# Seven block products instead of eight in the down product of an MLP, with the sums of token tiles made on GpSimd

## The reference, cut to what matters

```
for i in range(2):
    ...
    u = rms_norm(x, g_mlp[i])                                   # 256 x 1024
    x = x + jnp.square(jax.nn.relu(u @ w_ff1[i])) @ w_ff2[i]    # 1024 -> 4096 -> 1024
```

## Time and profile before

| | before |
|---|---|
| median of the runs | 798.21 us |
| the profiled execution, its own time | 798.14 us |
| its span, first to last instruction | 796.3 us |
| PE busy | 789.5 us (99%) |
| PE weight loads busy | 658.7 us (83%) |
| VectorE busy | 530.0 us (67%) |
| ScalarE busy | 425.1 us (53%) |
| GpSimd busy | 106.9 us (13%) |

### The profile page before, as it was taken

The page is one execution under the profiler, slowest core; times in us unless marked ns, Lnnn a source line. Parts: engine busy times, 40 slices in busy tenths (PEclk is TensorE's granted clock), DMA queues, the critical chain, the costliest instruction groups (busy, mean ns, idle before and its releaser), DMA issues.

```text
span 796.3 us, 11076 instructions
## 1 busy us (share of the span) xinstructions
PE 789.5 (99%) x4150; PEld 658.7 (83%) x4150; DVE 530.0 (67%) x709; ACT 425.1 (53%) x615; POOL 106.9 (13%) x136
## 2 busy tenths in 40 slices
PE   8999999999999999999999999999999999999998
PEld 7998977778888778888888888887778888888886
DVE  6657987767676677576655656678766756666561
ACT  6646655654755564464444454548674545534440
POOL 0500300000130410030000000078900000000000
PEclk9999999999999999999999999999999999999999
DMA  9961463447656634546665565461424566656541
GB/s 344 352 201 40 159 198 121 142 156 287 221 196 201 208 106 149 169 158 213 212 208 175 194 207 170 151 212 54 134 79 159 170 215 223 220 178 208 172 144 53
DMA packets 76230, 142.52 MB, mean 179 GB/s; under 512 B 2928, under 2 KB 21504, under 8 KB 76064
## 3 DMA queue, kind: packets, MB, share of 16 engines
q1 hardware_dynamic: 74128, 135.08, 50.9%
q0 software_dynamic: 1776, 6.84, 2.5%
q10 hardware_dynamic: 288, 0.10, 0.0%
HBM read 140.95 MB, written 1.05 MB: 178 GB/s over the span
## 4 chain that ended last, share of the span: by engine, by line
PE 97%; DVE 1%; ACT 1%; DMA 0%; issue 0%; ACTq 0%; DVEq 0%
PE bank L1776 60%; PE bank L2154 15%; PE bank L2160 7%; PE bank L1949 2%; PE bank L2017 2%; PE bank L1864 2%; PE bank L1798 1%; PE bank L1831 1%; PE bank L1917 1%; PE bank L1991 1%; PE bank L2223 1%; PE bank L1790 1%; PE bank L1997 1%; DMA proj<-in_opening 0%; PE bank L2213 0%
## 5 line engine op out<-in xcount | busy, mean ns | idle before, releaser
L1776 PE MATMUL bank<-w_hi,a_both 128*128 128x512 f32 (+2 forms) x720 | 226.3, 384 | 0.1
L1193 DVE TENSOR_TENSOR w_lo<-raw,w_hi 128x2048 fp32r<-128x2048 f32 (+2 forms) x67 | 152.5, 2277 | 63.2 <-ACT w_hi L712 61.5
L1657 DVE TENSOR_TENSOR w_lo<-raw,w_hi 128x2048 fp32r<-128x2048 f32 x48 | 110.0, 2292 | 90.6 <-ACT w_hi L1095 89.6
L2154 PE MATMUL bank<-a_both,w_hi 128*128 128x512 f32 x512 | 163.2, 396 | 0.0
L712 ACT ACTIVATE w_hi<-raw 128x2048 fp32r<-128x2048 f32 (+2 forms) x67 | 125.9, 1879 | 68.0 <-PE bank L1776 31.2
L1776 PEld LDWEIGHTS bank<-w_hi,a_both 128*128 128x128 f32 x720 | 134.6, 188 | 22.0 <-issue 1.7
L1095 ACT ACTIVATE w_hi<-raw 128x2048 fp32r<-128x2048 f32 x48 | 92.0, 1917 | 112.4 <-PE bank L1776 51.0
L1776 PE MATMUL bank<-w_hi,b_hi 128*128 128x512 f32 x376 | 148.6, 395 | 0.1
L1776 PE MATMUL bank<-w_lo,b_hi 128*128 128x512 f32 x376 | 146.5, 390 | 0.0
L1776 PE MATMUL bank<-w_hi,b_lo 128*128 128x512 f32 x376 | 146.5, 389 | 0.0
L1776 PE MATMUL bank<-w_lo,a_both 128*128 128x512 f32 (+2 forms) x360 | 135.9, 378 | 0.0
(11 more groups left out here) (236 smaller groups left out, 820.4 us busy)
## 6 DMA issues: line engine op xcount, KB each, us to landing
raw<-in_w_ff SPq DMA_DIRECT2D x64, 1024.0 KB, 5.1
raw<-in_w_in_moba SPq DMA_DIRECT2D x20, 512.0 KB, 4.5
raw<-in_w_merge SPq DMA_DIRECT2D x8, 1024.0 KB, 5.0
raw<-in_w_out SPq DMA_DIRECT2D x8, 1024.0 KB, 5.1
m<-in_w_in SPq DMA_DIRECT2D x6, 880.0 KB, 9.3
raw<-in_w_mem_kv SPq DMA_DIRECT2D x4, 1024.0 KB, 5.2
raw<-in_w_ple_gate SPq DMA_DIRECT2D x4, 1024.0 KB, 5.1
raw<-in_w_in_pool SPq DMA_DIRECT2D x4, 1024.0 KB, 5.1
```

The source lines that it names most:

```text
L1193: dve.tensor_tensor(w_lo[:, v % RING, 0:n], landing[land_slot(v)][:, 0:n], w_hi[:, v % RING, 0:n].bitcast(F32), ALU.subtract).then_inc(lo_ ...
L1657: dve.tensor_tensor(w_lo[:, (base + c) % RING, :], raw[:, (base + c) % RAW, :], w_hi[:, (base + c) % RING, :].bitcast(F32), ALU.subtract). ...
L1776: ins = pe.matmul(banks[t][:, 0:n], xa[:, kt, ts], wa[:, slot, w], start=first and k == 0 and q == 0, stop=last and k == kts - 1 and q == 2)
L2154: return pe.matmul(b_hid[f][:, :].rearrange("p (q n) -> p q n", q=2), w_hi[:, slot, w], a_both[:, kt], start=kt == 0, stop=kt == KT - 1)
```

## The change: what it does

**Pairs.** The middle of each MLP (chunks 0 to 6 of the down product) is cut into 14 pairs of k-tiles: pair (c, h) has 256 hidden values and all 1024 outputs. One unit of the up product makes two columns of 128 hidden values of the next chunk, another unit holds the pair's down weights, as four pieces of 512 columns, B00, B01, B10, B11 (the first digit is the k-tile, the second the half of the outputs). The weights are laid out for this ahead of the launch, so that each unit is one plain transfer.

**Seven products.** With the token tiles t0 and t1 and the two k-tiles, the pair's product is a 2 x 2 block product. 10 of 14 pairs in each MLP (h = 1 in every chunk, h = 0 in chunks 1, 3 and 5; in_sums names them) make it of seven block products. For that VectorE makes differences of the weight pieces (differences: one instruction of 1024 columns, two of 512), ScalarE and VectorE split these too (sum_hi, sum_lo, 1536 columns), and GpSimd makes four sums of tiles of hidden values (token_sums). The results accumulate in banks 0, 2, 3, 5, 6, 7 and 1, and stay there until the end of the MLP. The other four pairs have eight products, in the same banks with two differences of token tiles.

**Up product woven in.** Seven banks are taken, so one is left for the up product: bank 4. PE makes one column of 128 hidden values at a time (up_columns, 16 instructions); ScalarE copies the whole bank (512 columns, into halves, which lies in memkv) and VectorE adds the halves from there. PE's order in a pair: first column, first half of the down products, second column, second half. The second column waits until ScalarE has copied the first (ff_part).

**End.** Chunk 7 has the old form. VectorE adds the extra banks up (flush) before PE's last unit and adds them to x.

**Buffers.** In the MLPs four landing buffers are used (two of them lie in m), rot_tab moves into proj. prob and probT hold the differences.

The core of the diff:

```diff
+            def token_sums(lay):
+                for n in range(FF):
+                    for h in range(2):
+                        gp.wait_ge(ff_relu, 2 * FF * lay + 2 * n + h + 1)
+                        tile = [tok[:, h, j * P:j * P + P] for j in range(7)]
...
+                        elif in_sums((U_FF1 if lay else U_FF0) + 3 + 4 * n + 2 * h):
+                            gp.tensor_tensor(tile[4], tile[1], tile[3], ALU.add).then_inc(*link.step())
+                            gp.tensor_tensor(tile[6], tile[0], tile[1], ALU.subtract).then_inc(*link.step())
+                            link.wait()
+                            link(gp.tensor_tensor(tile[5], tile[4], tile[0], ALU.subtract))
+                            gp.tensor_tensor(tile[1], tile[2], tile[5], ALU.subtract).then_inc(ff_sq, 1)
...
+                def hidden_hi(n, h):
+                    act.wait_ge(ff_sq, 2 * FF * lay + 2 * n + h + 1)
...
+                def split_sums(v, between):
+                    i, e = sums_up_to(v), ext_of(v)
+                    act.wait_ge(diffs_made, i)
+                    act.wait_ge(unit_used, v - RING + 2)
+                    act.activation(sum_hi[e][:, 0:2 * CB], diff_13, ACT.Copy).then_inc(diffs_hi, 1)
+                    between()
+                    act.activation(w_hi[:, v % RING, :], landing[land_slot(v)], ACT.Copy).then_inc(diffs_hi, 1)
+                    act.activation(sum_hi[e][:, 2 * CB:3 * CB], diff_2, ACT.Copy).then_inc(hi_ready, 1)
...
+                for c in range(TP):                                       # ScalarE
+                    for h in range(2):
+                        copy_halves(c + 1, 2 * h + 1)
...
+                        unit(base + 6 + 4 * c + 2 * h - LOOK)
+                        hidden_hi(c + 1, h)
+                        nxt = (c + 1, 2) if h == 0 else (c + 2, 0)
+                        down(base + 7 + 4 * c + 2 * h, lambda: copy_halves(*nxt))
...
+                for c in range(TP):                                       # VectorE
+                    for h in range(2):
+                        ahead = base + 7 + 4 * c + 2 * h
+                        if c < TP - 1:
+                            differences(ahead)
+                        hidden_pair(c + 1, h)
...
+                        unit(ahead - 1 - LOOK)
+                        hidden_lo(c + 1, h)
+                        down(ahead)
...
+                def products_of(u):
+                    if in_sums(u):
+                        return [(5, 0, 1), (0, 2, 0), (2, 1, 3), (1, 3, 2), (3, 4, 4), (6, 5, 6), (7, 6, 5)]
+                    return [(0, 0, 1), (1, 1, 1), (2, 4, 2), (3, 1, 2), (0, 2, 0), (1, 3, 0), (2, 5, 3), (3, 3, 3)]
...
+                for c in range(TP):                                       # PE
+                    for h in range(2):
...
+                            half_of(0)
+                            up_columns(u, c, 2 * h + 1)
+                        half_of(1)
```

More of the change, by code:

```diff
@@ L51 @@
 FF = 8
+TP = FF - 1
+SUMS = ((1, 3, 5), tuple(range(7)))
 REACH = 16
@@ L185, with layer_of, mlp_unit, in_sums @@
 GAIN_PRE, GAIN_MIX, GAIN_MEM, GAIN_MLP, GAIN_HEAD = 0, 8, 24, 40, 56
+def layer_of(u):
+    return int(u >= U_FF1)
+def mlp_unit(u):
+    return u - (U_FF1 if u >= U_FF1 else U_FF0) if U_FF0 <= u < U_MOBA0 or u >= U_FF1 else None
+def in_sums(u):
+    r = mlp_unit(u)
+    return r is not None and 3 <= r < 4 * FF - 2 and r % 2 == 1 and (r - 3) // 4 in SUMS[(r - 3) // 2 % 2]
+def sums_up_to(u):
+    return sum(in_sums(v) for v in range(U_FF0, u + 1))
 def build(nc, a, out):
@@ L284, in build @@
         head_tmp = (m[:, 0:2 * S], m[:, 8 * S:10 * S])
-        rot_tab = m[:, 4 * S:6 * S].rearrange("p (w t c d) -> p w t c d", w=2, t=NT, c=2)
-        hidden = tok[:, 0, :].rearrange("p (k n) -> p k n", k=4)
+        rot_tab = proj[:, 12 * CB:13 * CB].rearrange("p (w t c d) -> p w t c d", w=2, t=NT, c=2)
+        halves = memkv[:, 0, :, :]
+        diff_13, diff_2 = prob[:].rearrange("p t n -> p (t n)"), probT[:, 0:CB]
+        flush_m1, flush_u2 = diff_13[:, 0:CB], diff_13[:, CB:2 * CB]
+        flush_w, flush_u3 = probT[:, 0:CB], probT[:, CB:2 * CB]
+        sum_hi, sum_lo = [sums[:, 0, j, :] for j in range(2)], [sums[:, 1, j, :] for j in range(2)]
+        tiles_hi, tiles_lo = (b[:].rearrange("p k n -> p (k n)") for b in (b_hi, b_lo))
         raw_landed = [sem(f"raw_landed{i}") for i in range(RAW_IN)]
@@ new lines, in down @@
+                def down(v):
+                    if not in_sums(v):
+                        unit(v - LOOK)
+                        return
+                    i, e = sums_up_to(v), ext_of(v)
+                    dve.wait_ge(diffs_hi, 2 * i - 1)
+                    dve.tensor_tensor(sum_lo[e][:, 0:2 * CB], diff_13, sum_hi[e][:, 0:2 * CB].bitcast(F32), ALU.subtract)
+                    dve.wait_ge(diffs_hi, 2 * i)
+                    dve.tensor_tensor(w_lo[:, v % RING, :], landing[land_slot(v)], w_hi[:, v % RING, :].bitcast(F32), ALU.subtract)
+                    dve.wait_ge(hi_ready, v + 1)
+                    dve.tensor_tensor(sum_lo[e][:, 2 * CB:3 * CB], diff_2, sum_hi[e][:, 2 * CB:3 * CB].bitcast(F32), ALU.subtract)\
+                       .then_inc(lo_ready, 1)
@@ L2159, in low @@
                         kt, w = 4 * half_ + k, slice(k * CB + f * P, k * CB + f * P + P)
-                        return pe.matmul(b_hid[f][:, 0:S], w_lo[:, slot, w], a_hi[:, kt, :], start=False, stop=False)
-                    for one, two in banked + pairs if read is not None else pairs + banked:
+                        return pe.matmul(bank[4 + f][:, 0:S], w_lo[:, slot, w], a_hi[:, kt, :], start=False, stop=False)
+                    for one, two in pairs + banked:
                         high(*one)
@@ L2174, in up, with up_columns, high, low @@
                     ins.then_inc(unit_used, 1)
+                def up_columns(u, c, f):
+                    b = bank[5 if c == 0 and f == 1 else 4]
+                    g, slot = f % 2, u % RING
+                    if g == 0:
+                        pe.wait_ge(lo_ready, u + 1)
+                    pe.wait_ge(ff_part, 4 * FF * lay + ((1, 2, 5, 7)[f] if c == 0 else 4 * (c + 1) + f))
+                    def high(kt):
+                        return pe.matmul(b, w_hi[:, slot, g * D + kt * P:g * D + kt * P + P],
+                                         a_both[:, kt].rearrange("p q n -> p (q n)"), start=kt == 0, stop=kt == KT - 1)
+                    def low(kt):
+                        return pe.matmul(b[:, 0:S], w_lo[:, slot, g * D + kt * P:g * D + kt * P + P], a_hi[:, kt, :],
+                                         start=False, stop=False)
+                    for kt in range(0, KT - 2, 2):
+                        high(kt)
+                        high(kt + 1)
+                        low(kt)
+                        low(kt + 1)
+                    high(KT - 2)
+                    low(KT - 2)
+                    low(KT - 1)
+                    ins = high(KT - 1)
+                    ins.then_inc(unit_used if g else ff_up, 1)
```

287 lines of the change are left out of this document (168 added, 119 removed).

## The result

| | before | changed |
|---|---|---|
| median | 798.27 us (4 runs) | 892.09 us (4 runs, 890.2 to 892.72) |
| profiled execution | 798.14 us | 890.2 us |
| its span | 796.3 us | 888.2 us |

The changed kernel is slower by a ratio of 1.117, 95% interval 1.115 to 1.119. The forecast was 870, the range 815 to 890. The measured time lies 22 us above the forecast and 2 us above the range. The direction and the mechanism of the turns were right; the sum came out too small at the starts and the ends of the MLPs and between them.

What follows compares the result with a forecast made beforehand. PE bounded the kernel before; with the change a ring of VectorE, GpSimd and ScalarE sets the pace. 36.1 us more per MLP, 72.2 for two, on 798.2 gives 870 us, range 815 to 890.

Steps and rivals of the forecast that it cites:

- the first turn's E: In a pair's turn, the end of ScalarE's b_hi behind GpSimd's sums; the first was put at T + 25.9.
- eleven turns: Middle of each MLP: 8 turns of 15.2 us and 3 of 9.7, together 150.7 us.
- A seven: A pair with seven block products: a turn of 15.2 us, with 10.3 us of PE work.
- an eight: A pair with eight block products: a turn of 9.7 us, with 11.0 us of PE work.
- this ring: In the MLP turns, VectorE, GpSimd and ScalarE wait for each other and set the pace, 15.2 us; chance 0.66.
- The hold: In each turn, GpSimd's sums can't start beside VectorE's w_lo; the first works only from 0.15 us before its end.
- Not held: Rival: GpSimd gets its reads in beside VectorE's w_lo; 11.4 us more per MLP, 821 us; chance 0.14.
- Start-up: From PE's first up column to the first E in each MLP: 25.9 us.
- The sum for one MLP: Per MLP, start, turns and end: 25.9, 150.7 and 19.2, together T + 195.8; before 159.7, so 36.1 us more.
- moved buffers, landing and flush at nothing: Around the MLPs: these cost nothing; if uncovered, a landing some 5 us and flush's additions 2.8 us per MLP.
- a clock that stays low: Rival: PE's stops in the turns keep it at 1.2 GHz, some 960 to 1010 us; chance 0.06.
- Keeps pace: Rival: VectorE's waits in the turns get hidden and PE alone sets the end, say 790 us; chance 0.09.

Runs made afterwards that it cites:

- experiment 1: The changed kernel with one wait added, so that VectorE waits for GpSimd's sums before the up unit's w_lo: 847.42 us, ratio 1.061.
- the second kernel of experiment 4: The changed kernel with VectorE's b_lo a turn later, ScalarE's b_hi behind the weights, and 14 pairs of seven products, every second pair: 812.9 us, ratio 1.019.
- experiment 8: Four kernels, against the changed one: b_lo a turn later, table behind sums, ten or twelve sevens, none in a row, different ends: 801.59, 803.77, 799.39, 798.66 us.
- the first of 4: The changed kernel with its 20 sevens kept, VectorE's b_lo a turn later and ScalarE's b_hi behind the weights: 832.3 us, ratio 1.043.
- the last kernel: The kernel with twelve sevens (799.39 us), with the end's first w_lo moved between VectorE's second and third reads of the flushed banks: 798.66 us, ratio 1.0005.
- experiment 5: The changed kernel with ScalarE copying the next pair's first column ahead of b_hi instead of behind it: 873.04 us, ratio 1.095.
- experiment 2: The changed kernel with VectorE making the sums of token tiles itself behind the square, GpSimd's part empty: 828.55 us, ratio 1.039.

## Why the prediction missed: the mechanism held, two steps of its sum failed

Each mark is the start of an instruction, T the start of PE's first up column (342.64 and 678.79 us):

| step | predicted | MLP 0 | MLP 1 |
|---|---|---|---|
| start to the first turn's E | 25.9 | 28.8 | 26.0 |
| eleven turns | 150.7 | 150.8 | 151.6 |
| from there to the end | 19.2 | 22.9 | 23.1 |
| one MLP against before (159.7) | +36.1 | +42.8 | +41.0 |
| between the MLPs | 0 | +8.1 | |

The whole is +91.9 on the span, predicted 72.2. Of the 19.7 us between them, 18.7 lie at the starts, at the ends and between the MLPs, and 1.0 in the turns. The upper end of the range, 890, allowed for slower sums on GpSimd alone (+18 us) and had nothing for the ends.

- **One turn.** Right in its size and in its parts. A seven took 15.3 us behind another seven (15.2 predicted); VectorE's idle times were 2.81 and 1.00 (2.9 and 1.0). From b_lo to b_lo an eight came 10.7 to 11.8 behind a seven, where the prediction's parts give 6.2 + 1.4 + 3.7 = 11.3, and a seven 13.7 to 14.1 behind an eight, where they give 4.6 + 2.6 + 1.4 + 5.0 = 13.6. A cycle of four took 55.4 (once 56.2) for 55.3. "PE is nowhere in this ring" holds between sevens only: at the eight the copy waits for PE, as in this line, and the chain that ended last runs through PE there (499.70 to 508.34). That the eight still fits is in part luck, since its waits lie elsewhere than the prediction put them.

```profile
453.04 0.60 ACT L1112 ACTIVATE memkv<-bank 128x512 f32<-128x512 f32 x1 [1.10 <-PE bank L2290]
```

- **A sum of 128 columns on GpSimd.** 0.45 to 0.47 alone, by the line through the earlier trace rows. The estimate of 0.28 from the Trainium skill (GPSIMD Engine Reference, Performance versus the Vector engine) was too low; the rows stood nearer.

- **The hold.** The earlier trace rows carried it, and experiment 1 shows it. "Not held", 821 us, is out.

- **Start-up.** 25.9 was right for MLP 1. In MLP 0 GpSimd's table stood ahead of the first sums; the 5.61 us of GpSimd in the first line of the earlier trace rows were that table, and I had written GpSimd off as idle:

```profile
341.80 4.46 POOL L726 TENSOR_TENSOR proj<-rope_m,head_gain 128x32 f32<-128x32 f32 x16
346.34 0.74 POOL L715 TENSOR_TENSOR tok<-tok 128x256 f32<-128x256 f32 x1
347.12 0.85 ACT L1120 ACTIVATE b_hi<-tok 128x768 fp32r<-128x768 f32 x1 [5.17 <-POOL tok L715]
```

- **The first failed step: the end of "The sum for one MLP".** After the last E I let the copy come at 8.9 and PE do one column and nine products behind it. The chain in order of time shows what PE still had to do from the copy on, in its own order, start and length:

```profile
526.74 2.74 PE bank L2337 x12
...
532.27 2.74 PE bank L2337 x12
...
537.83 0.61 ACT memkv L1112
```

  Two blocks of 12 products and three columns of about 2.8 us stand there before PE's last column is ready to be copied. That column starts at 535.00, 12.8 behind the last E, where the sum has 8.9. The term is 22.9 for 19.2: 3.7 in MLP 0 and 3.9 in MLP 1.

- **The second failed step: moved buffers, landing and flush at nothing.** Between the MLPs it is 8.1 us. The chain of the changed kernel after VectorE's last reads:

```profile
544.67 2.08 DVE x L1746 x3
...
546.78 2.30 DVE w_lo L1252
549.10 0.37 SPq L537
...
549.51 5.01 DMA raw<-in_w_in_moba
554.54 1.92 ACT w_hi L750
556.48 2.29 DVE w_lo L1252
558.77 0.80 DVE a_both L1264 x2
...
559.71 2.32 PE bank L1883 x9
```

  The x additions and two w_lo stand before the addition for which PE waits (a stop of 4.64 us), and a landing of 5.0 us stands behind the first of them. PE's second stop is 1.24, and between the two its clock was low (0.50 over the first 4 us): the instructions from the transposes on take 5.65 in place of 3.65 before the change, which costs 2.0. That is 7.9 of the 8.1. I had argued that the DMA share, 0.59 and falling, hides any landing. But a share says nothing of a transfer that can't start: its buffer was freed late. My price of 5 us for it, if the cover went, was of the right size.

- **PE's clock.** Behind 12 of the 18 stops in the turns it fell and came back, as these stretches of the changed kernel show, ahead of a stop, behind it, and 4.5 us later:

```profile
432.00:438.90 6.90, 6.90 (x35) 5.51 (x33) 6.69 (x8) 1.78 (x1) 1.75 (x1) 1.00 0.44 152
443.50:447.70 4.20, 4.17 (x15) 3.60 (x16) 3.20 (x3) 2.30 (x2) 0.00 (x0) 0.59 0.01 4
448.00:452.80 4.80, 4.80 (x26) 4.12 (x25) 3.77 (x4) 3.26 (x3) 0.74 (x1) 1.00 0.62 218
```

  At 0.59 for 4.2 us, most of it at the low level of 1.2 GHz, PE loses 1.7. Behind the other 6 stops (at 428.29, 523.67, 721.55, 761.69, 817.84 and 857.92) the clock stayed at 1.00 over the next 4 us. So the rule of the Trainium skill (TensorE: Matmul & The Clock Gate, HAM oscillation), the low clock at every group, held at 12 of 18 groups and not at each. As the prediction said, the turn hides it: the turn up to 443.53, at 1.00 behind its stop, took 15.24 us, and others, behind whose stops the clock fell, 15.3. PE's busy time holds 32 us of it (18.6 more, though 13.6 of work went). The rival of a clock that stays low is out: 0.92 over the MLPs.

- **Keeps pace.** Out for this kernel. Its condition, mean turns under 11.0 us with the waits hidden, was reached by the second kernel of experiment 4 (10.83) and by 8 with other orders and fewer sevens, not by the first of 4 with the same 20 sevens (11.48); the 790 us of the rival weren't, for the reasons at the end of experiment 8.

What stays open: why a seven saves 0.44 and not 0.68 where PE has no visible stop. In the last kernel PE loses 0.22 us once per seven, at its second column (440.11 to 441.16 for four products that take 0.91 elsewhere, and 0.53 for 0.45 behind them). That adds up to 0.66. The column starts 0.15 us behind the end of ScalarE's copy (440.43, 0.58 long), which stands behind b_hi, and b_hi had waited 5.32 us for GpSimd's last sum. So the copy is the likely wait, but no experiment moved it. Open is also why moving the copy saves 3 us at the end of each MLP in experiment 5.

## What to carry to other kernels

When work leaves the bound engine, write the turn of the others as a ring, with who waits for whom, before counting what is saved. An idle engine isn't a free one: put a step of the ring on the engine where it is shortest, or move its user a turn later, so that nothing waits for it. Check the ends of the loop as carefully as its middle: 18.7 of the 19.7 us that the forecast missed lay there, and for each transfer ask which instruction frees its buffer, not how busy the queues are.

## What the runs showed of the hardware that was not expected

- VectorE's w_lo holds back small GpSimd instructions almost to its end: one of 128 columns took 2.44 us beside a 2.28 us VectorE instruction, 0.46 without. Where GpSimd was first, its instruction of 128 columns ran in 0.47 and only the next was held, 2.51 us (350.46 and 350.88 in the changed kernel).
- VectorE does 128 columns in 0.29, GpSimd in 0.46.
- Behind stops of 1.5 us PE went on at the full clock (first kernel of experiment 4: 1.00 over the next 4 us), behind 2.85 us the next 2.9 us were granted 0.65 on the mean, behind 3.88 us the next 3.9 us 0.50, and behind 4.59 us the next 4.2 us 0.59. But the length of the stop alone doesn't decide: behind five stops of 2.25 us in the changed kernel the clock fell three times and stayed at 1.00 twice, and behind one of 1.76 us in experiment 2 (728.19) the next 4 us had 0.64.
